# Expert layers of a two-block model: 37 panels of each layer's weights land in six buffers beside the ring of eight

## The reference

```python
def ec_moe(h, w_router, w_gate, w_up, w_down):        # h: (1, 512, 1024), 16 experts of width 1024
    cap = max(1, EC_FACTOR * n // N_EXPERTS)          # 64 tokens for each expert
    aff = softmax(h @ w_router)
    gate, idx = lax.top_k(jnp.swapaxes(aff, 1, 2), cap)          # each expert picks its 64 tokens
    xs = jax.vmap(lambda hb, ib: hb[ib])(h, idx)
    a = silu(xs @ w_gate) * (xs @ w_up)               # for each expert its own 1024 x 1024 matrices
    out = (a @ w_down) * gate[..., None]
    return scatter_add(out, idx)
```

## Time and profile before

| | us |
|---|---|
| median of 3 runs | 3561.61 (3548.75 to 3563.95) |
| the profiled execution | 3550.22 |
| its span | 3548.4 |
| TensorE busy | 3128.6 (88%) |
| VectorE busy | 1156.7 (33%) |
| ScalarE busy | 895.5 (25%) |
| DMA queue of SyncE (q1) | 627 MB, 47.3% of 16 engines' span |
| chain that ended last | TensorE 10%, DMA 5%, VectorE 2% |

### The profile page before, as it was taken

How to read it: one execution, slowest core, us unless ns; L and a number is a source line. 1 busy time by engine, 2 the same in 40 slices (tenths; PEclk the granted TensorE clock), 3 DMA queues, 4 the chain that set the end, 5 groups by cost and what they waited for, 6 DMA issues and landing times. The chain is left out here.

```text
span 3548.4 us, 39560 instructions
## 1 busy us (share of the span) xinstructions
PE 3128.6 (88%) x17458; PEld 2114.2 (60%) x17458; DVE 1156.7 (33%) x1634; ACT 895.5 (25%) x1354; POOL 0.2 (0%) x4
## 2 busy tenths in 40 slices
PE   5987789999897888999999987888899976889997
PEld 3765767888665776888677666643433343343442
DVE  3446533232536543223342347410000046000002
ACT  3443132232444223223343521210000032100001
POOL 0000000000000000000000000000000000000000
PEclk8998989999998889999999988999999997999999
DMA  7224112222234302232452000499999930999996
GB/s 251 83 85 180 58 44 87 97 97 92 75 105 158 107 1 71 95 98 92 141 200 71 13 1 1 153 393 405 400 382 404 397 120 24 380 401 393 380 401 248
DMA packets 247386, 637.14 MB, mean 180 GB/s; under 512 B 12848, under 2 KB 110128, under 8 KB 247088
## 3 DMA queue, kind: packets, MB, share of 16 engines
q1 hardware_dynamic: 244128, 627.22, 47.3%
q10 hardware_dynamic: 3088, 7.40, 0.6%
HBM read 632.48 MB, written 2.10 MB: 179 GB/s over the span
## 5 line engine op out<-in xcount | busy, mean ns | idle before, releaser
L575 PE MATMUL ps<-mix_halves,work_halves 128*128 128x512 f32 (+1 forms) x1544 | 622.6, 403 | 39.6 <-DVE h_halves L2066 30.6
L575 PE MATMUL ps<-h_halves,work_halves 128*128 128x512 f32 (+1 forms) x1544 | 609.2, 395 | 4.4 <-ACTq L1444 2.3
L575 PE MATMUL ps<-mix_halves,ring_halves 128*128 128x512 f32 x1448 | 567.4, 392 | 0.0
L575 PE MATMUL ps<-ring,work 128*64 128x512 f32 x2048 | 460.8, 598 | 73.4 <-DMA ring<-in_w_exp_gate 52.4
L2066 DVE TENSOR_TENSOR ring_halves<-ring,work_halves 128x2048 fp32r<-128x2048 f32 (+2 forms) x125 | 252.6, 2021 | 544.5 <-ACT work_halves L1453 449.4
L575 PEld LDWEIGHTS ps<-ring,work 128*64 128x64 f32 x2048 | 155.6, 137 | 371.2 <-issue 370.8
L575 PEld LDWEIGHTS ps<-mix_halves,work_halves 128*128 128x128 f32 (+1 forms) x1544 | 291.2, 189 | 126.9 <-issue 42.3
L575 PEld LDWEIGHTS ps<-h_halves,work_halves 128*128 128x128 f32 (+1 forms) x1544 | 291.8, 189 | 72.3 <-issue 6.4
L575 PEld LDWEIGHTS ps<-mix_halves,ring_halves 128*128 128x128 f32 x1448 | 271.8, 188 | 60.5
L1453 ACT ACTIVATE work_halves<-ring 128x2048 fp32r<-128x2048 f32 x102 | 188.2, 1846 | 425.7 <-PE ps L575 333.3
L575 PE MATMUL ps<-ring,proj 128*64 128x512 f32 (+1 forms) x1664 | 265.9, 525 | 27.1 <-ACT proj L1927 17.8
(11 more groups left out here) (371 smaller groups left out, 3239.1 us busy)
## 6 DMA issues: line engine op xcount, KB each, us to landing
ring<-in_w_exp_gate SPq DMA_DIRECT2D x128, 1024.0 KB, 9.5
ring<-in_w_exp_up SPq DMA_DIRECT2D x128, 1024.0 KB, 13.0
ring<-in_w_exp_down SPq DMA_DIRECT2D x128, 1024.0 KB, 11.6
ring<-in_ada_w SPq DMA_DIRECT2D x48, 1024.0 KB, 7.6
ring<-in_w_mod SPq DMA_DIRECT2D x48, 1024.0 KB, 7.6
ring<-in_w_in SPq DMA_DIRECT2D x22, 1024.0 KB, 5.1
ring<-in_w_gate SPq DMA_DIRECT2D x22, 1024.0 KB, 5.1
ring<-in_w_up SPq DMA_DIRECT2D x22, 1024.0 KB, 5.1
```

What stands on the lines that cost most here:

```text
L575: i = pe.matmul(o, lhsT, rhs, start=start, stop=stop, **kw)
```

## The change

In each expert layer, panels from the ninth on may also land in six further places of 2048 floats: four in the buffer of the pair outputs, usable for panels of pairs up to 0, 2, 4 and 6, since the outputs of pairs 0 and 1, 2 and 3 and so on are written there; two in `h`, up to pair 0. A panel takes the open place whose last panel is the oldest, one without a panel first. SyncE waits until the panel there before has been read; for the first use in a layer it waits for the router logits (the four places of y), or for the eight copies of tokens (the two of h). Each place has its own semaphore, which TensorE and ScalarE wait for. So that h stays dead through pair 0, the gate tiles are turned in pairs 1 and 2, not in 0 and 1.

```diff
+SPARE = (("y", 0, 0), ("y", 2048, 2), ("y", 4096, 4), ("y", 6144, 6), ("h", 0, 0), ("h", 2048, 0))
-        slot_in = [ctx.enter_context(nc.semaphore(f"slot_in{r}")) for r in range(RING)]
+        slot_in = [ctx.enter_context(nc.semaphore(f"slot_in{r}")) for r in range(RING + len(SPARE))]
...
+        seat, follows, landing = [], [], []
+        last, uses = [None] * (RING + len(SPARE)), [0] * (RING + len(SPARE))
+        for n in range(len(panels)):
+            layers = [l for l in range(2) if 8 <= n - expert_start[l] < 12 * E]
+            open_ = list(range(RING))
+            for l in layers:
+                pair_ = (n - expert_start[l]) // 24
+                open_ += [RING + i for i, (_, _, until) in enumerate(SPARE) if pair_ <= until]
+                for i in range(RING, RING + len(SPARE)):
+                    if last[i] is not None and last[i] < expert_start[l]:
+                        last[i] = None
+            r = min(open_, key=lambda i: (-1 if last[i] is None else last[i]))
+            seat.append(r)
+            follows.append(last[r])
+            last[r] = n
+            uses[r] += 1
+            landing.append(uses[r])
+
         def slot(n):
 
             _, k, width = panels[n]
-            return cut(ring, n % RING * PANEL, k * width, k=k, n=width)
+            if seat[n] >= RING:
+                where, start, _ = SPARE[seat[n] - RING]
+                return cut(proj_all if where == "y" else hflat, start, k * width, k=k, n=width)
+            return cut(ring, seat[n] * PANEL, k * width, k=k, n=width)
+
+        def landed(n):
+            return slot_in[seat[n]], 16 * landing[n]
...
-        gate_tiles = {0: (0, 1), 1: (2, 3)}
+        gate_tiles = {1: (0, 1), 2: (2, 3)}
...
             for n, (src, k, width) in enumerate(panels):
-                if n >= RING:
-                    sp.wait_ge(sem["panel_used"], n - RING + 1)
-                sp.dma_start(slot(n), src).then_inc(slot_in[n % RING], 16)
+                if follows[n] is not None:
+                    sp.wait_ge(sem["panel_used"], follows[n] + 1)
+                elif seat[n] >= RING:
+                    l = int(n >= expert_start[1])
+                    if SPARE[seat[n] - RING][0] == "y":
+                        sp.wait_ge(sem["r_logits"], l + 1)
+                    else:
+                        sp.wait_ge(sem["r_tok_sb"], 8 * (l + 1))
+                sp.dma_start(slot(n), src).then_inc(slot_in[seat[n]], 16)
...
-                pe.wait_ge(slot_in[n % RING], 16 * (n // RING + 1))
+                pe.wait_ge(*landed(n))
```

More of the change, by code:

```diff
@@ L476, in build @@
                 by_rows(a["w_down"][l], FB, half)
+        expert_start = []
         def expert_panels(l):
+            expert_start.append(len(panels))
             for e in range(0, E, 2):
@@ L1451, in split_panel @@
                 n = halved[splits[0]]
-                act.wait_ge(slot_in[n % RING], 16 * (n // RING + 1))
+                act.wait_ge(*landed(n))
                 to("hi", f(rounded(panel_high(splits[0])), slot(n), ACT.Copy))
@@ L1497, in split_block @@
                 src, hi = even_block(s)
-                act.wait_ge(slot_in[even_blocks[s][0] % RING], 16 * (even_blocks[s][0] // RING + 1))
+                act.wait_ge(*landed(even_blocks[s][0]))
                 to("hi", f(rounded(hi), src, ACT.Copy))
```

## The result

The changed kernel takes 3510.8 us (3492.0 to 3512.8, 4 runs) against 3561.8 for the one before: a ratio of 0.9857, 95% interval 0.9828 to 0.9887, or 51 us less (40 to 61). Run again twice with others it came to 0.9864 (0.9842 to 0.9887) and 0.9888 (0.9866 to 0.9910), 48 and 40 us. The forecast was 3519, 42.5 us less.

What follows compares the result with a forecast made beforehand. The prediction took DMA as the bound in pairs 0 to 2, side by side with TensorE in pairs 3 to 7. 15.2 + 30.3 - 3 = 42.5 us off the median 3561.61 gave 3519, range 3504 to 3536.

Steps and rivals of the forecast that it cites:

- Head start, second layer: Ahead of the second expert layer, six panels flow under the router before the first gate: 15.4 us gained.
- Second layer in all: Second expert layer, head start and stalls together: its end moves from 3524.65 to 3494.4, 30.3 us less.
- the 3: Both expert layers: 3 us taken off the gain for some 10 places where a panel's release is barely in time.
- The walk through the pairs: Both layers, pair by pair: each gate, up, down ends at TensorE's own time or 3.5 us after its last panel's due.
- First layer: First expert layer: no head start, stalls removed, the end moves from 2849.25 to 2834.0, 15.2 us less.
- the later 11.9: First layer, from panels 26 and 27 to 174 and 175: 11.9 us of stalls, measured 390.8 against 378.9.
- Gate tiles: Turning the gate tiles in pairs 1 and 2 instead of 0 and 1: same work one pair later, 0 us.
- Rate of the new places: Panels landing in y or h flow at the ring's 2.56 us a panel, and TensorE reads them at the same pace.
- Rival (c): Both layers: panels landing in y or h flow slower; at 1 us more each, 3593 us. Chance 0.03.
- Rival (a): Inside the layers, stalls return as spare places close; only 15 to 27 us gained, 3540 us. Chance 0.15.
- Rival (b): Early panels are handed back, as TensorE behind its last combine sets the layer's end: gain 0, 3562 us. Chance 0.04.
- (d): Both layers: no stall at all and a little more at the ends, 48 us gained, 3514 us. Chance 0.1.

## Why the prediction was right

**Head start, second layer, 15.4 us.** Right: six panels, 2972 to 2990, without delay to the router (37.4 us from logits to first gate, 37.5 before). Panel 14's transfer starts where panel 8's did. The measured 14 us between the version without head start and the change are this, less the 1.3 us of DMA time lost at 3045 to 3050, which that version doesn't lose.

**Second layer in all, 30.3 us less its share of the 3.** Right in kind and size: 28.0 us (509.5 to 481.5, means of three profiles each). The walk through the pairs can be checked place by place. From the first gate, pairs 1 to 7 were to start after 51.0, 106.8, 162.6, 229.2, 290.8, 348.9 and 410.2 us; they start after 50.8, 106.4, 164.4, 229.8, 292.3, 350.5 and 411.9. The waits stand where they were put, in the gates of pairs 3, 6 and 7, with 1 us more in pair 4's and 0.27 us in pair 2's, where none was forecast. The one place named as short, panel 28 after panel 16 by 1.1 us, is the stretch at 303 GB/s: 1.3 us. Pair 3 starts 1.8 us late because of a term that the walk does not have, the clock in pair 2:

```profile
3131.29 5.67 PE L609 MATMUL ps<-proj,work 128*64 128x512 f32 x17 [1.16 <-issue]
```

The same 17 instructions took 4.03 us in pair 1. The granted clock of 3131 to 3137 is 0.72, after waits of 0.27, 1.41 and 1.16 us around the gate tiles, and so it is in this place in all three profiles of the change. It costs the layer nothing here, as the next gate waits for panels anyway.

**First layer, 15.2 us less the rest of the 3.** Right in kind, too much by some 3: 12.4 from router to end, 11.7 from first gate (means of three profiles each), and 497.4 us of length where 493 was written. The early 3.3 us are gone in full (panel 27 is used 118.1 us after the transfers begin near 2285.9, 121.5 us before, from near 2281.1). Of the later 11.9, 10.3 are. Of the 1.6 that are left, 1.0 lies in two stretches of the profile after:

```profile
2580.00:2585.00 5.00, 5.00 (x26) 1.67 (x24) 0.00 (x0) 0.00 (x0) 0.00 (x0) 1.00 0.94 369
2640.00:2645.00 5.00, 5.00 (x26) 1.61 (x24) 0.00 (x0) 0.00 (x0) 0.00 (x0) 1.00 0.98 370
```

They are the downs of pairs 3 and 4, the places "98 after 88" and "122 after 112". The 8 us of lead that a panel needs put the breaks in the right places and within 0.3 us of their size. The 3 us taken off for all of them were too few: the walk gives 45.5 us without them, and 39.7 are measured in the two layers (11.7 and 28.0, from first gate to end), where 42.5 were forecast.

**Gate tiles, 0 us.** Nearly right for the change, but not for the reason given: the count of the work is the same, yet in the kernel before the tiles in pair 0 cost the DMA some 2 us. Beside the spare places they cost next to nothing, wherever they stand. What this leaves wrong is the start of the walk. It took 3044.39, the use of the eighth panel in the trace of before, as the date on which an unbroken stream brings it; that use was late by 1.9 us, by TensorE's turning of the tiles and the late issue. In the second layer this error and the breaks and small delays that were not counted pull against each other, so that a walk that meets the trace within 2 us at each pair owes part of that to luck.

**Rate of the new places.** Rival (c) is refuted: where nothing breaks the stream it is at 408 to 410 GB/s (2985 to 2990 after, 3045 to 3050 without the head start), and 409 in most slices of the two layers of the page after, with 37 panels of each layer in y and h. TensorE reads them at the pace of the ring (3.60 for 16). The Trainium skill, "SBUF — State Buffer", section "Who interferes with whom", says that DMA never contends with a compute engine; no row here speaks against it, though TensorE reads `proj` while panels land in it. The stream keeps 409 GB/s, above the 358 of the page that the prediction weighed, so the reckoning by which no stall would matter does not hold here.

**Rival (a)** was half right and in the wrong place. Closing places do hand a lead back: 12 us of DMA time in pair 0, when all six close after one panel each. In the change three close with pair 0 and the others two pairs apart, and the breaks are 1.3 us and less. **Rival (b)**, no gain, is refuted by the 28 us of the second layer, and (d), 48 us with no stall left, is what the first two timed comparisons say but not the layers, which give 40 and still have breaks.

**What is open.** The three timed comparisons say 51, 48 and 40 us, the layers 40. The last agrees; the two others hold 40 only at the edge of their intervals. That the first comes out beyond the 34 to 50 of the forecast's own range is thus not the layers' doing. For the second and third, the clocks of the runs say more. Within one comparison an execution is some 3 us shorter for each 0.001 of mean granted clock (2.2 to 3.9 in the four sets of runs). The means were 0.9470 before and 0.9490 after in the second comparison, 0.9488 and 0.9497 in the third. By an estimate from these numbers, 6 of the 48 us and 3 of the 40 are clock and not the change, which leaves 42 and 37. Why one execution has more of the lower clock ahead of the layers than the next stays open.

## What to carry to other kernels

When transfers bound a stage, count the lost time of the queue, not the waits of the engine, and ask of each loss whether it is a late start or a break because no buffer is free. A lead built ahead of a stage lasts only as long as there are buffers to hold it: a head start and room later were worth 8 and 27 us alone and 40 together. Work out for each transfer which release it follows, and compare that with its due time; the walk over eight pairs came out within 2 us at each step, with some luck.

## What was not expected of the hardware

Nothing in the rates: with the queue fed, one core's stream held 409 GB/s for 450 us. What surprised was the spread between equal executions: the first logits of the first expert layer started between 2276.0 and 2295.7 us in six of them, with mean granted clocks of 0.948 to 0.952 and 249 to 283 us at the lower clock ahead of the layers, while the two layers behind repeated within 2.2 and 0.7 us in each kernel.
